# Attention scores from rounded high and low parts of queries and keys, split inside the scan stage

## The reference, cut to what matters

```python
def one_block(args):                       # a block of 128 queries
    qn_b, qr_b = args
    s = (jnp.einsum('bqhd,bkhd->bhqk', qn_b, k_nope)
         + jnp.einsum('bqhd,bkd->bhqk', qr_b, k_rope))
    p = jax.nn.softmax(s.astype(jnp.float32) * scale, axis=-1)
    return jnp.einsum('bhqk,bkhd->bqhd', p.astype(v.dtype), v)
...
def step(state, inp):                      # the recurrence, forwards and backwards
    r_t, w_t, k_t, v_t, a_t, b_t = inp
    sa = jnp.einsum('bhvk,bhk->bhv', state, a_t)
    state = (state * w_t[:, :, None, :] + sa[..., None] * b_t[:, :, None, :]
             + v_t[..., None] * k_t[:, :, None, :])
    return state, jnp.einsum('bhvk,bhk->bhv', state, r_t)
```

## Time and profile before

| | us |
|---|---|
| median of 3 runs (3155.31 to 3159.33) | 3156.21 |
| the profiled execution | 3153.93 |
| its span, first to last instruction | 3152.1 |
| PE busy over the span | 3069.7 (97%) |
| DVE / ACT / POOL busy | 2026.5 (64%) / 1136.5 (36%) / 448.5 (14%) |
| scan stage, S(0) to the start of the last scores | 522.3 to 1137.7 |
| scores on PE in it (L1784, busy) | 125.9 |

### The profile page before, as it was taken

The page is one execution under the profiler, slowest core; times in us unless marked ns, Lnnn a source line. Parts: engine busy times, 40 slices in busy tenths (PEclk is TensorE's granted clock), DMA queues, the critical chain, the costliest instruction groups (busy, mean ns, idle before and its releaser), DMA issues.

```text
span 3152.1 us, 52318 instructions
## 1 busy us (share of the span) xinstructions
PE 3069.7 (97%) x22008; PEld 2495.9 (79%) x22008; DVE 2026.5 (64%) x3073; ACT 1136.5 (36%) x1691; POOL 448.5 (14%) x488
## 2 busy tenths in 40 slices
PE   8999999899999999999999999999999999999999
PEld 7887887677777777888888888888766887788887
DVE  6665554477777765546555565788887888664454
ACT  5222334566666653223222222201154233433232
POOL 0232442011111100402222212101000000200000
PEclk9999999999999999999999999999999999999999
DMA  4332766223232222425455553666411222223322
GB/s 151 127 133 84 229 224 205 67 78 95 78 93 73 81 99 92 154 86 220 175 197 196 195 200 134 253 240 264 176 67 54 94 97 90 94 94 121 107 94 80
DMA packets 121754, 424.98 MB, mean 135 GB/s; under 512 B 15536, under 2 KB 41776, under 8 KB 94128
## 3 DMA queue, kind: packets, MB, share of 16 engines
q1 hardware_dynamic: 86880, 295.26, 26.6%
q0 software_dynamic: 34640, 126.37, 10.9%
HBM read 311.48 MB, written 110.10 MB: 134 GB/s over the span
## 4 chain that ended last, share of the span: by engine, by line
PE 81%; DVE 11%; issue 2%; ACT 2%; POOL 2%; DMA 1%; SPq 0%; DVEq 0%; ACTq 0%; POOLq 0%
PE ps L2634 30%; PE ps L321 14%; PE ps L505 7%; PE ps L2442 4%; PE ps L1784 3%; PE ps L2344 3%; PE ps L1417 2%; PE ps L2158 2%; PE ps L1379 1%; DVE st_m L1813 1%; PE ps L1433 1%; PE ps L1795 1%; PE ps L2801 1%; PE ps L1026 1%; DVE Yh L2823 1%
## 5 line engine op out<-in xcount | busy, mean ns | idle before, releaser
L293 ACT ACTIVATE whi<-raw 128x2048 fp32r<-128x2048 f32 x131 | 250.5, 1912 | 389.0 <-PE ps L2634 195.3
L297 DVE TENSOR_TENSOR wlo<-raw,whi 128x2048 fp32r<-128x2048 f32 x131 | 301.7, 2303 | 86.0 <-ACT whi L293 85.7
L2823 DVE SCALAR_TENSOR_TENSOR Yh<-uT,vc,Yh 128x512 f32<-128x512 f32 x448 | 326.2, 765 | 3.2
L2634 PE MATMUL ps<-Hh,whi 128*128 128x512 f32 x1024 | 316.9, 391 | 0.6 <-DVE wlo L297 0.6
L2634 PEld LDWEIGHTS ps<-Hh,whi 128*128 128x128 f32 x1024 | 192.2, 188 | 42.5 <-issue 1.9
L321 PE MATMUL ps<-Hlo,whi 128*128 128x512 f32 x672 | 206.9, 389 | 0.0
L321 PE MATMUL ps<-Hhi,wlo 128*128 128x512 f32 x672 | 206.9, 389 | 0.0
L321 PE MATMUL ps<-Hhi,whi 128*128 128x512 f32 x672 | 206.8, 389 | 0.0
L2634 PE MATMUL ps<-aHh,whi 128*128 128x512 f32 x512 | 199.5, 390 | 2.3 <-DVE wlo L297 2.2
L2634 PE MATMUL ps<-Hh,wlo 128*128 128x512 f32 x512 | 199.2, 389 | 0.0
L2634 PE MATMUL ps<-aHh,wlo 128*128 128x512 f32 x512 | 199.2, 389 | 0.0
(11 more groups left out here) (415 smaller groups left out, 6470.0 us busy)
## 6 DMA issues: line engine op xcount, KB each, us to landing
raw<-in_panels SPq DMA_DIRECT2D x131, 1024.0 KB, 4.8
whi<-sph SPq DMA_DIRECT2D x28, 1024.0 KB, 4.8
wlo<-spl SPq DMA_DIRECT2D x28, 1024.0 KB, 6.9
rwf<-F POOLq DMA_DIRECT2D x16, 1280.0 KB, 6.7
sraw<-in_panels POOLq DMA_DIRECT2D x40, 512.0 KB, 4.5
sph<-shi POOLq DMA_DIRECT2D x40, 512.0 KB, 4.5
spl<-slo POOLq DMA_DIRECT2D x40, 512.0 KB, 5.2
L<-rwf SPq DMA_DIRECT2D x16, 1024.0 KB, 5.0
```

The costliest lines, as they stand in the source:

```text
L293: e.activation(whi[i % 2][:, :], raw_of(i)[:, :], AF.Copy).then_inc(*a_hi.up(i))
L297: e.tensor_tensor(wlo[i % 2][:, :], raw_of(i)[:, :], whi[i % 2][:, :].bitcast(F32), OP.subtract).then_inc(*v_lo.up(i))
L2634: m = e.matmul(ap, W[wi][:, kc, n0:n0 + 128], mov[mi][:, kc, :], start=x == 0 and q == 0, stop=x == len(kcs) - 1 and q == 2)
L2823: e.scalar_tensor_tensor(out=to, in0=x, scalar=w, in1=to, op0=OP.mult, op1=OP.add).then_inc(*v_e.up(*key))
```

## The change

The scores become three products of float32r parts. A head's keys have a buffer of their own: `Khi[h]` (rounded copy) and, in the next 4 KB, `Kraw[h]` (as loaded) and `Klo[h]` (the difference), the last two at the same address, so the split overwrites the raw keys. There is one such pair for each h, and a head pair's keys are loaded only when the last scores with the former ones are done (head 0 after S(16k - 2), head 1 after S(16k - 1)). Queries have two sets of `Qhi` and `Qraw`/`Qlo` in place of three `Qb`.

Added to ACT are 8 key copies (`k_act`, L1771) and 32 query copies (`q_act`, L1790), to DVE 8 and 32 subtractions (`k_dve`, L1775, and `q_dve`, L1794). S(u) on PE has six matmuls in place of two, and waits for the DVE subtraction in place of the landing. The query load g is issued at unit 2g - 2 in place of 2g - 4. Values keep their two buffers.

```diff
-    Kp = [sb(f"Kp{i}", 8 * i, [96, 2, S]) for i in range(2)]
+    Khi = [sb(f"Khi{h}", 8 * h, [96, S], F32R) for h in range(2)]
+    Kraw, Klo = [sb(f"Kraw{h}", 8 * h + 4, [96, S]) for h in range(2)], [sb(f"Klo{h}", 8 * h + 4, [96, S], F32R) for h in range(2)]
...
-    Qb = [sb(f"Qb{i}", 174 + i, [96, 2, 128]) for i in range(3)]
+    Qhi = [sb(f"Qhi{i}", 174 + 2 * i, [96, 2, 128], F32R) for i in range(2)]
+    Qraw, Qlo = ([sb(f"Qraw{i}", 175 + 2 * i, [96, 2, 128]) for i in range(2)],
+                 [sb(f"Qlo{i}", 175 + 2 * i, [96, 2, 128], F32R) for i in range(2)])
...
+    def k_sp(e, k, h):
+        if k:
+            e.wait_ge(*t_at.by("S", 16 * k - 2 + h))
+        e.dma_start(Kraw[h][:, :], qkd[1, :, 2 * k + h, :]).then_inc(*d_kp.up(k, h))
...
+    def k_act(e, k, h):
+        e.wait_ge(*d_kp.by(k, h))
+        e.activation(Khi[h][:, :], Kraw[h][:, :], AF.Copy).then_inc(*a_at.up("Khi", k, h))
+
+    def k_dve(e, k, h):
+        e.wait_ge(*a_at.by("Khi", k, h))
+        e.tensor_tensor(Klo[h][:, :], Kraw[h][:, :], Khi[h][:, :].bitcast(F32), OP.subtract).then_inc(*v_at.up("Klo", k, h))
+
+    def vp_sp(e, k):
         if k >= 2:
-            e.wait_ge(*t_at.by("S", 16 * k - 17))
             e.wait_ge(*t_at.by("O", 8 * k - 9))
-        e.dma_start(Kp[k % 2][:, :, :], qkd[1, :, 2 * k:2 * k + 2, :]).then_inc(*d_kp.up(k))
         e.dma_start(Vp[k % 2][:, :, :], vds[:, :, 128 * k:128 * (k + 1)]).then_inc(*d_vp.up(k))
...
     def q_sp(e, g):
         k, j = g // 8, g % 8
-        if g >= 3:
-            e.wait_ge(*t_at.by("S", 2 * g - 5))
-        e.dma_start(Qb[g % 3][:, :, :], qkd[0, :, 2 * k:2 * k + 2, 128 * j:128 * (j + 1)]).then_inc(*d_qb.up(g))
+        if g >= 2:
+            e.wait_ge(*t_at.by("S", 2 * g - 3))
+        e.dma_start(Qraw[g % 2][:, :, :], qkd[0, :, 2 * k:2 * k + 2, 128 * j:128 * (j + 1)]).then_inc(*d_qb.up(g))
+
+    def q_act(e, g):
+        e.wait_ge(*d_qb.by(g))
+        e.activation(Qhi[g % 2][:, :, :], Qraw[g % 2][:, :, :], AF.Copy).then_inc(*a_at.up("Qhi", g))
+
+    def q_dve(e, g):
+        e.wait_ge(*a_at.by("Qhi", g))
+        e.tensor_tensor(Qlo[g % 2][:, :, :], Qraw[g % 2][:, :, :], Qhi[g % 2][:, :, :].bitcast(F32),
+                        OP.subtract).then_inc(*v_at.up("Qlo", g))
...
     def att_pe(e, u, c):
         g, k, j, h = u // 2, u // 16, (u // 2) % 8, u % 2
         if c == "S":
-            if u % 16 == 0:
-                e.wait_ge(*d_kp.by(k))
+            if u % 16 == h:
+                e.wait_ge(*v_at.by("Klo", k, h))
             if h == 0:
-                e.wait_ge(*d_qb.by(g))
+                e.wait_ge(*v_at.by("Qlo", g))
             if u:
                 e.wait_ge(*a_at.by("E", u - 1))
-            for half in range(2):
-                m = e.matmul(bank[4 + half], Qb[g % 3][:, h, :], Kp[k % 2][:, h, hs(half)], start=True, stop=True)
+            for q, (Qx, Kx) in enumerate(((Qhi, Khi), (Qhi, Klo), (Qlo, Khi))):
+                for half in range(2):
+                    m = e.matmul(bank[4 + half], Qx[g % 2][:, h, :], Kx[h][:, hs(half)], start=q == 0, stop=q == 2)
             m.then_inc(*t_at.up("S", u))
...
         if c == "M":
             e.wait_ge(*t_at.by("S", u))
             e.tensor_reduce(st_m[:, u:u + 1], ps[:, 2048:3072], AX, OP.max, negate=True).then_inc(*v_at.up("max", u))
+            if u % 2 and u // 2 + 1 < 32:
+                q_dve(e, u // 2 + 1)
+            if u == 0:
+                k_dve(e, 0, 1)
         if c == "R":
             e.wait_ge(*a_at.by("E", u))
             e.reciprocal(st_r[:, u:u + 1], st_s[:, u:u + 1]).then_inc(*v_at.up("rec", u))
+            if u % 16 == 15 and u < 63:
+                k_dve(e, (u + 1) // 16, 0)
+            if u and u % 16 == 0:
+                k_dve(e, u // 16, 1)
...
@@ -1828,9 +1860,15 @@
                 e.wait_ge(*t_at.by("PT", u - 2, 1))
             e.activation(Pb[u % 2][:, :], ps[:, 2048:3072], AF.Exp, bias=st_m[:, u:u + 1],
                          accum_out=st_s[:, u:u + 1]).then_inc(*a_at.up("E", u))
+            if u % 16 == 15 and u < 63:
+                k_act(e, (u + 1) // 16, 0)
+            if u and u % 16 == 0:
+                k_act(e, u // 16, 1)
         if c == "P":
             e.wait_ge(*v_at.by("rec", u))
             e.activation(Pb[u % 2][:, :], Pb[u % 2][:, :], AF.Copy, scale=st_r[:, u:u + 1]).then_inc(*a_at.up("P", u))
+            if u % 2 == 0 and u // 2 + 1 < 32:
+                q_act(e, u // 2 + 1)
         if c == "C1":
...
     def att_sp(e, u, c):
         if c == 0 and u < 64:
-            if u % 2 == 0 and u // 2 + 2 < 32:
-                q_sp(e, u // 2 + 2)
+            if u % 2 == 0 and u // 2 + 1 < 32:
+                q_sp(e, u // 2 + 1)
             if u % 16 == 5 and 1 <= u // 16 < 3:
-                kv_sp(e, u // 16 + 1)
+                vp_sp(e, u // 16 + 1)
+            if u % 16 >= 14 and u < 62:
+                k_sp(e, u // 16 + 1, u % 2)
...
     def scan_dve(e):
+        k_dve(e, 0, 0)
         pre_over(e)
+        q_dve(e, 0)
         scan(e, "dve", w_dve, att_dve, tail_dve)
 
     def scan_act(e):
+        k_act(e, 0, 0)
         pre_over(e)
+        q_act(e, 0)
+        k_act(e, 0, 1)
         scan(e, "act", w_act, att_act, tail_act)
...
-        kv_sp(e, 0)
+        k_sp(e, 0, 0)
         e.wait_ge(*v_lo.by(WO - 1))
-        kv_sp(e, 1)
+        k_sp(e, 0, 1)
+        vp_sp(e, 0)
+        vp_sp(e, 1)
...
-        for k in range(2):
-            q_sp(e, k)
+        q_sp(e, 0)
```

More of the change, by code:

```diff
@@ L1755, in build @@
     Oh = [sb(f"Oh{i}", 170 + 2 * i, [128, 512]) for i in range(2)]
-    Qb = [sb(f"Qb{i}", 174 + i, [96, 2, 128]) for i in range(3)]
+    Qhi = [sb(f"Qhi{i}", 174 + 2 * i, [96, 2, 128], F32R) for i in range(2)]
+    Qraw, Qlo = ([sb(f"Qraw{i}", 175 + 2 * i, [96, 2, 128]) for i in range(2)],
+                 [sb(f"Qlo{i}", 175 + 2 * i, [96, 2, 128], F32R) for i in range(2)])
     oas = dram("oas", [4, 128, S])
     t_at, v_at, a_at = signals("t_at"), signals("v_at"), signals("a_at")
-    d_kp, d_vp, d_qb, d_oa = landings("d_kp", 2), landings("d_vp", 2), landings("d_qb", 3), landings("d_oa", 2)
-    def kv_sp(e, k):
+    d_kp, d_vp, d_qb, d_oa = landings("d_kp", 2), landings("d_vp", 2), landings("d_qb", 2), landings("d_oa", 2)
+    def k_sp(e, k, h):
[9 more added lines that the diff above has]
+    def vp_sp(e, k):
         if k >= 2:
-            e.wait_ge(*t_at.by("S", 16 * k - 17))
             e.wait_ge(*t_at.by("O", 8 * k - 9))
-        e.dma_start(Kp[k % 2][:, :, :], qkd[1, :, 2 * k:2 * k + 2, :]).then_inc(*d_kp.up(k))
         e.dma_start(Vp[k % 2][:, :, :], vds[:, :, 128 * k:128 * (k + 1)]).then_inc(*d_vp.up(k))
```

## The result

| | before | after |
|---|---|---|
| median, 15 runs each on one chip | 3158.25 | 3162.51 |
| lowest to highest | 3150.22 to 3165.77 | 3159.96 to 3169.94 |
| span of the profiled execution | 3152.1 | 3161.0 |
| granted clock over that span | 0.992 | 0.989 |
| PE / DVE / ACT busy | 3069.7 / 2026.5 / 1136.5 | 3056.0 / 2046.5 / 1152.1 |

The ratio after to before is 1.002, 95% interval 1.001 to 1.0029: about 6 us slower, where the forecast was 0.6 us faster (3155.6) with a range of 3142 to 3168 that holds the time. PE is busy 14 us less and the kernel takes 6 us more, so PE's own work is not where the time went.

The account below looks back on a forecast made before the run. It took a chain of waits, mostly through PE but leaving it for DVE and ACT, as the bound. Terms -7.2 + 5.9 + 2.6 - 1.6 + 0.9 - 1.2 = -0.6 us took the median 3156.21 to 3155.6, range 3142 to 3168.

Parts of the forecast that it names:

- a rival with a chance of 0.2: PE's granted clock falls behind added waits at the start and new head pairs; 3163.6, range 3160 to 3168, chance 0.2.
- the steady cycle: Eight units, 20 to 27: -1.2 us a cycle, to about 78.8; six cycles from 624.59 to 1107.15 give -7.2.
- the new head pairs: Units 16, 32, 48: PE stands 1.96 us each for the key subtraction behind R(16k - 1); +5.9 us in all.
- head 1's split: At new head pairs, behind unit 16k: lands in ACT and DVE idle time before S(16k + 1); 0.
- S shorter by 0.40: Each S on PE: six float32r matmuls take 1.46 us in place of 1.86, so 0.40 less.
- S on the chain in five of eight places: Steady cycle: S(20), S(21), S(22), S(24), S(26) count 0.40 each; S(23), S(25), S(27) gain nothing.
- Query splits on the chain, +0.34 and +0.45: Steady cycle: Qlo behind M(23) adds 0.34; Qhi and Qlo behind S(26) together add 0.45.
- Start: S(0) waits for the first key and query splits: S(0) 3.2 us later, S(1) 2.6 to 2.7; counted as +2.6.
- Unit 10's load: Query load lands at 613.0, so ACT waits 3.4 us and the V starts 1.1 later; about +0.9 handed on.
- Up to 624: First units: S(1), S(3), S(4), S(7), S(9) each 0.40 shorter, Qlo behind M(1) takes 0.34 back; -1.6.
- End: Last units: S(60) to S(62) gain as in the steady cycle, S(63) is off the chain; -1.2.
- Idle time of PE where S is off the chain: Ahead of L1433 behind S(25) and L1807 behind S(22), PE's idle time goes up by 0.4.

Follow-up runs that it names:

- gain_only: Changed kernel with the splits and loads behind the start left out, the six products per S kept; ratio 0.9965 to the kernel before.
- start_ahead: Changed kernel with both heads' first keys and the first queries split ahead of the last gate's work; ratio 1.0027 to the kernel before.

## Why the prediction was wrong

**The step that failed** is in the rivals: "Against it: the 2.49 us wait lay in thin work, those at units 16 to 48 lie in dense work." The sum counted each wait of PE that it added or lengthened at its length, and gave the slower matmuls behind it to a rival with a chance of 0.2. They came at the start (S(0) to S(1) 5.96 in place of 4.61 us), behind two in three of the waits for the keys, at 613, and behind the waits that the query splits had lengthened (at 944 and 1109). From S(12) to S(60) falls and holes make some 5 to 8 us in the two profiles of the changed kernel; that of the kernel before has none there.

It is not the whole miss. From S(12) to S(60) the terms themselves, without falls, came to some +2 us where the sum had -1.3. Two were mis-sized: the steady cycle, -4.4 for -7.2, and the new head pairs, where head 1's split was put at nothing.

The rival's mechanism was right. That its 3163.6 lies so near the median of 3162.51 is in part luck: it had two or three drops of up to 5 us, and the runs have more and smaller ones, 0.6 to 1.6 us each from S(12) on, on top of terms that were too low.

Step by step:
- **S shorter by 0.40**: the six products were 1.49 to 1.59 to the next start where PE goes on without a gap, not 1.46, against 1.81 to 1.91 before, and count 0.32 each in the cycle. Mis-sized: the last step leads to another kind of matmul (0.56, not 0.46).
- **S on the chain in five of eight places**: right; gain_only's -1.61 is 5 x 0.32, not 8 x 0.32.
- **Query splits on the chain, +0.34 and +0.45**: right in size (+0.88 together, 0 when moved), though behind S(26) the chain ends over ACT, which the prediction had ended over DVE. That end is the wait at L1347, 1.23 us where before had 0.27, and 1.95 where it had 0.99: the sum priced the splits at their push and not at what a longer wait of PE brings.
- **A cycle of 78.8 us**: 79.14, so -0.7 in place of -1.2. Taken for all six cycles, as the sum did, -4.4 in place of -7.2.
- **New head pairs +1.96**: S(16k - 1) to S(16k) grew by 1.98, 1.88 and 1.97, the waits are 1.8. But head 1's split, put at 0, is +0.3 (S(32) to S(33) 11.50, where gain_only has 11.20), and the clock behind the wait 1.3 two times in three.
- **Start**: S(0) at 525.35, forecast 525.5. S(1) at 531.31, forecast 529.6: the clock, at its lower level from 525 to 535.
- **Unit 10's load**: issued 610.17, ACT's wait 3.80 (forecast 3.4), the V slow behind it.
- **Up to 624**: S(12) +1.24, forecast +1.9, by luck: before's profile had a slow stretch at 580 to 590 us that after's had not. This hid the start's loss in a comparison of two profiles.
- **End** -1.2: S(60) to S(63) -0.66.
- **Idle time of PE where S is off the chain**, forecast up by 0.4: ahead of L1433 behind S(25) 0.34 from nothing, ahead of L1831 (the L1807 of before) behind S(22) 0.84 from 0.51.

## What to carry to other kernels

When a change makes PE wait where it had not, or makes a wait longer, price the wait at its length and at the slow matmuls behind it, in dense work too: here 1.8 us of standing cost 1.94 and on average 0.9 more. Work that is added off the bounding engine costs what its place costs: the same splits were 0.9 us a cycle between P and C1 and behind M, and nothing 2.3 and 2.7 us later. Where runs spread by 0.3%, a mean granted clock beside each time helps to see what goes with the clock, but one slope for two kernels can mislead: here the sign at the same clock hung on it. Held against it, the shortest time of each piece over several profiles shows what the code takes without falls.

## What the runs showed of the hardware

- In dense work the clock fell behind waits of 1.22 to 1.30 us at 6 of 28 places, of 1.80 to 2.14 us ahead of S(16k) at 12 of 18, of 1.95 us behind S(51) and S(59) at 11 of 14, and behind waits of 0.99 us or less at L1347 at none of 44. It stayed low for some 3 us. Where idle matmuls filled the wait of 1.8 us it fell at none of three places.
- Starting earlier can be worth nothing: start_ahead's S(0) came 3.2 us sooner, PE ran at the lower level from 524 to 541 us, and nothing was left of it.
- Beside a POOL subtraction of 2.36 us a DVE product with two SBUF operands took 2.79 us in place of 0.68.
- 43 matmuls that compute nothing made the kernel before 0.31% faster, about as much as the best rearranged forms of the change without them (0.35 and 0.26%); with both kernels filled the two can't be told apart (0.9960 and 0.9969).
- Holes of 0.58 to 1.21 us in PE with no wait behind them stand in 11 of the 17 profiles between S(0) and S(63), six times behind S(36) and five behind S(28); in the other six profiles there is none of them. Their cause is open.
